# Block 1's projections from x times the norm's weight, with 1/std at the evictions, and the neighbourhood attention's values head by head in column halves

## What is computed

```
# block 1
h = x * rsqrt(mean(x*x, channels) + eps) * mix_norm_g
q, k, v, g, u, sv = split(h @ w_in)             # 4 heads of 128 and 4 groups of 128
q, k = rotary(q), rotary(k)
ret = silu(g) * rmsnorm(retention(q, k, v))     # chunks of 128 positions
sgu = gelu(u) * (w_s @ layernorm(gelu(sv)) + b_s)
x = x + concat(ret, sgu) @ w_out                # then a feed-forward part

# block 2, neighbourhood attention: 8 heads of 64, a grid of 16 rows and 64 columns
for each grid row r (64 queries):
    p = softmax(q_row @ k_window.T * scale + bias)   # 8 rows of 64 keys
    out[r] = p @ v_window
```

## Time and profile before

| | us |
|---|---|
| median of 3 runs (3180.71 to 3182.11) | 3181.14 |
| the profiled execution | 3180.48 |
| its span, first to last instruction | 3179.2 |
| TensorE busy | 3003.6 (94%) |
| VectorE busy | 1780.6 (56%) |
| ScalarE busy | 1150.5 (36%) |

### The profile page before, as it was taken

How to read it: one execution, slowest core, us unless ns; L and a number is a source line. 1 busy time by engine, 2 the same in 40 slices (tenths; PEclk the granted TensorE clock), 3 DMA queues, 4 the chain that set the end, 5 groups by cost and what they waited for, 6 DMA issues and landing times.

```text
span 3179.2 us, 34027 instructions
## 1 busy us (share of the span) xinstructions
PE 3003.6 (94%) x13986; PEld 2355.1 (74%) x13986; DVE 1780.6 (56%) x2535; ACT 1150.5 (36%) x1708; POOL 2.2 (0%) x6
## 2 busy tenths in 40 slices
PE   7999798999999997999998989999988899999997
PEld 5887687888888875877775757665556688888885
DVE  4442336444454447676774453667663866666666
ACT  3223413222222225344445434555642522222223
POOL 0000000000000000000000000000000000000000
PEclk9999999999999998999999999999989999999999
DMA  3211011111111111111110111000001111111111
GB/s 136 79 59 44 30 47 40 47 47 48 52 49 51 44 49 34 40 40 33 34 33 20 33 33 34 28 21 27 21 20 40 34 47 53 60 47 54 58 49 66
DMA packets 48823, 141.61 MB, mean 45 GB/s; under 512 B 12790, under 2 KB 16670, under 8 KB 48542
## 3 DMA queue, kind: packets, MB, share of 16 engines
q1 hardware_dynamic: 48670, 139.45, 14.0%
HBM read 135.16 MB, written 9.77 MB: 46 GB/s over the span
## 4 chain that ended last, share of the span: by engine, by line
PE 85%; ACT 6%; DVE 5%; issue 3%; DMA 0%; SPq 0%; ACTq 0%; DVEq 0%
PE psum L508 37%; PE psum L744 13%; PE psum L974 10%; PE psum L784 8%; PE psum L542 5%; PE psum L564 2%; PE psum L553 2%; PE psum L901 1%; PE psum L884 1%; PE psum L1056 1%; PE psum L1083 1%; PE psum L559 1%; DVE residual L1940 1%; ACT sb_left L1769 1%; DVE swa_p L2539 0%
## 5 line engine op out<-in xcount | busy, mean ns | idle before, releaser
L508 PE MATMUL psum<-h_hi,w_hi 128*128 128x512 f32 x1408 | 438.6, 393 | 6.6 <-ACT ret_q L1261 2.9
L508 PE MATMUL psum<-h_hi,w_lo 128*128 128x512 f32 x1408 | 434.0, 389 | 0.0
L508 PE MATMUL psum<-h_lo,w_hi 128*128 128x512 f32 x1408 | 434.0, 389 | 0.0
L1925 DVE TENSOR_TENSOR w_lo<-w_raw,w_hi 128x1024 fp32r<-128x1024 f32 x164 | 200.4, 1222 | 255.9 <-ACT w_hi L1168 255.5
L508 PEld LDWEIGHTS psum<-h_hi,w_hi 128*128 128x128 f32 x1408 | 262.8, 188 | 65.8 <-issue 13.0
L508 PEld LDWEIGHTS psum<-h_lo,w_hi 128*128 128x128 f32 x1408 | 264.3, 188 | 55.3
L508 PEld LDWEIGHTS psum<-h_hi,w_lo 128*128 128x128 f32 x1408 | 264.3, 188 | 55.2
L2166 DVE TENSOR_TENSOR residual<-residual,psum 128x1024 f32<-128x1024 f32 x176 | 214.5, 1219 | 141.6 <-PE psum L784 70.3
L1168 ACT ACTIVATE w_hi<-w_raw 128x1024 fp32r<-128x1024 f32 x164 | 172.5, 1052 | 227.3 <-PE psum L508 181.7
L974 PE MATMUL psum<-h_hi,w_hi 128*128 128x512 f32 x576 | 211.6, 447 | 5.2 <-ACT y L1180 2.3
L974 PE MATMUL psum<-h_hi,w_lo 128*128 128x512 f32 x576 | 204.1, 414 | 0.0
(11 more groups left out here) (332 smaller groups left out, 5256.4 us busy)
## 6 DMA issues: line engine op xcount, KB each, us to landing
w_raw<-in_weights SPq DMA_DIRECT2D x228, 512.0 KB, 3.5
residual<-in_x_t SPq DMA_DIRECT2D x8, 512.0 KB, 9.2
out_t<-residual SPq DMA_DIRECT2D x8, 512.0 KB, 3.0
rel_copies<-rel_rows SPq DMA_DIRECT2D x8, 480.0 KB, 6.2
na_bias<-rel_copies SPq DMA_DIRECT2D x8, 240.0 KB, 4.1
band_copies<-band_rows SPq DMA_DIRECT2D x8, 192.0 KB, 6.2
ret_rotary<-in_rotary SPq DMA_DIRECT2D x1, 1024.0 KB, 7.5
swa_bias<-band_copies SPq DMA_DIRECT2D x4, 256.0 KB, 2.8
```

The lines of the kernel that those rows point to most:

```text
L508: ins = self.pe.matmul(out[:, s], w[:, k, at:at + P], src(k, low)[:, s], start=(k == 0 and part == 0), stop=(k == n_k - 1 and part == 2))
L1925: self.dve.tensor_tensor(self.m.w_lo[:, n % 2, :], self.m.raw[:, n % 2, :], self.m.w_hi[:, n % 2, :].bitcast(F32), ALU.subtract).then_inc( ...
```

## The change

**First norm.** h_hi and h_lo are made from x * g, without 1/std, as x lands. The squares are summed over the eight tiles by VectorE; TensorE takes one mean of the sum (two matmuls, 4 passes) in the middle of tile 2. The loads start with the vectors and weight tiles 0 and 1; the constants come behind x. The rotary tables are multiplied by 1/std, and every other projection of block 1 is multiplied by 1/std by VectorE as it leaves PSUM; Silu and Gelu follow in place.

**Order.** Tiles 2 and 3 (v and gate of head 0) are projected straight behind the first pair, into banks 4 to 7. So head 0's three later projections are q, k and v of head 1, and head 1 has no value projection of its own at its start. VectorE multiplies the gate of heads 1 to 3 before it makes w_lo of the next tile.

**Values of the neighbourhood attention.** Each head is multiplied by itself, into its half of the partitions, and eight grid rows fill bank 7. ScalarE empties it with one operation.

```
 SyncE, program
+        sp.dma_start(m.vec[:], t["vectors"])
         for k in range(KD):
+            if k < 2: self.load_up_to(k)
             sp.dma_start(m.x[:, k, :], x[:, k, :])
+        sp.dma_start(m.common[:], t["common"])
         self.load_up_to(3); rotary; self.biases()
+        self.band()                      # was the end of biases()

 ScalarE, first_norm
+        self.split_up_to(0)
         for k in range(KD):
+            self.act.activation(m.h_hi[:, k, :], m.x[:, k, :], ACT.Copy, scale=m.v("mix_norm_g", k))
+            if k == 0: self.split_up_to(1)
+            if k > 2: q.wait_ge(*on("dve_n1_acc", k - 2))
             self.act.activation(dst[:], m.x[:, k, :], ACT.Square)
+        self.split_up_to(3)
         self.rsqrt(... m.n1_rstd, ("pe_n1_mean",), ("act_n1_rstd",))

 VectorE, first_norm
+        for k in range(KD):
+            self.dve.scalar_tensor_tensor(m.h_lo[:, k, :], m.x[:, k, :], m.v("mix_norm_g", k), m.h_hi[:, k, :], mult, subtract)
+            if k == 0: self.split_up_to(1)
+            if k > 1: self.add_first(k - 1)         # n_acc += squares
+        self.add_first(KD - 1)

 VectorE, retention
+        band add; self.split_up_to(3)
+        for n in range(2): m.rot[:, n, :] *= m.n1_rstd       # waits act_n1_rstd
         self.rotary(m.rq, 0, ...); self.rotary(m.rk, 1, ...)
+        self.values(0); self.times_rstd(m.rgate, 3, ("dve_rgate", 0))
         for h in range(RET_HEADS):
             t = 4 * h + 2
-            self.split_up_to(t + 1)
+            self.split_up_to(t + 1 if h else t + 2)
+            if h: self.values(h)                    # rt = proj t times 1/std
             rmask (waits pe_rscore); rqd
+            if h: self.times_rstd(m.rgate, t + 1, ("dve_rgate", h))
-            self.split_up_to(t + 2)
+            self.split_up_to(t + 2 if h else t + 3)
             state chain (waits pe_rkv) ...
             dve_rn (waits act_rrstd h); dve_ry

 TensorE, retention
         project_pair(...); band
+        for t, name in ((2, "dve_rv"), (3, "dve_rgate")):
+            out = self.take(("proj", t), 4 + 2 * (t - 2), 2, (name, 0))
+            for k in range(KD):
+                if t == 2 and k == 2: mean of m.n_acc into banks 6-7      # waits dve_n1_acc 7
+                ... six passes
         for h in range(RET_HEADS):
-            self.project(("act_rv", h))
+            if h > 1: self.project(("dve_rv", h))
             rkT, rscore, rvT (waits dve_rv h)
-            self.project(("act_rgate", h))
+            self.project(("dve_rgate", h) if h else ("dve_rq_cos", 1))
             rkv
+            self.project((q of h + 1) if h else ("dve_rk_cos", 1))
             ro
+            self.project((k of h + 1) if h else ("dve_rv", 1))
             rmean

 VectorE, gating
+                q.wait_ge(*on("pe_svT", g)); self.times_rstd(m.rk, t + 1, ("dve_sv", g + 1))
             smix; sy
+                self.after("dve_sy", g); self.times_rstd(m.rq, t, ("dve_u0", g + 1))

 TensorE, na_out
-        if r % 4 == 0: take bank 7
+        if r % 8 == 0: take bank 7
+        at = (r % 8) * GRID_W
         for b in range(4):
-            self.pe.matmul(self.n_out[:, (r % 4) * P:(r % 4 + 1) * P], m.nvtok[:, ks + 2 * b, :],
-                           m.npt[r % 2][:, b * P:(b + 1) * P], ...)
+            for a in range(2):
+                c = slice(64 * a, 64 * a + 64)
+                self.pe.matmul(self.n_out[c, at:at + GRID_W], m.nvtok[:, ks + 2 * b, c],
+                               m.npt[r % 2][:, b * P + 64 * a:b * P + 64 * a + 64], ...)

 ScalarE, na_out (every 8 rows, was every 4)
+        self.act.activation(m.y[:, p + 4, (r - 7) * GRID_W:(r + 1) * GRID_W], m.place["pe_nout", p, r // 8], ACT.Copy)
```

More of the change, by code:

```diff
@@ L603, in retention @@
         pe.matmul(out[0:SWA_HEADS, 0:REL_BAND], rel, onehot, start=True, stop=True).then_inc(*to("pe_band"))
+        for t, name in ((2, "dve_rv"), (3, "dve_rgate")):
+            q.wait_ge(*on("w_lo", t))
+            out = self.take(("proj", t), 4 + 2 * (t - 2), 2, (name, 0))
+            for k in range(KD):
+                if t == 2 and k == 2:
+                    q.wait_ge(*on("c_loaded"))
+                    q.wait_ge(*on("dve_n1_acc", KD - 1))
+                    mean = self.take(("pe_n1_mean",), 6, 2, ("act_n1_rstd", 1))
+                    for half, s in halves():
+                        pe.matmul(mean[:, s], m.c("mean1024"), m.n_acc[:, s], start=True, stop=True).then_inc(
+                            *to("pe_n1_mean", half))
+                w_hi, w_lo = self.weights(t)
+                for part, (w, low) in enumerate(((w_hi, 0), (w_lo, 0), (w_hi, 1))):
+                    for half, s in halves():
+                        ins = pe.matmul(out[:, s], w[:, k, :], self.h(k, low)[:, s], start=(k == 0 and part == 0),
+                                        stop=(k == KD - 1 and part == 2))
+            ins.then_inc(*to("proj", t))
+            self.tile += 1
         for h in range(RET_HEADS):
-            self.project(("act_rv", h))
+            if h > 1:
+                self.project(("dve_rv", h))
             q.wait_ge(*on("dve_rk", h))
@@ L1418, in neighbourhood @@
                 self.na_turn(step - 1)
-            if step >= 2 and (step - 2) % 4 == 3:
+            if step >= 2 and (step - 2) % 8 == 7:
                 self.na_out(step - 2)
@@ L2015, in retention @@
         dve.tensor_tensor(band, band, m.place[("pe_band",)][0:SWA_HEADS, 0:REL_BAND], ALU.add).then_inc(*to("dve_band"))
+        self.split_up_to(3)
+        q.wait_ge(*on("rotary_loaded"))
+        q.wait_ge(*on("act_n1_rstd", 1))
+        for n in range(2):
+            ins = dve.tensor_tensor(m.rot[:, n, :], m.rot[:, n, :], m.n1_rstd, ALU.mult)
+        ins.then_inc(*to("dve_rot"))
+        self.after("dve_rot")
+        self.rotary(m.rq, 0, "dve_rq", 0)
+        self.rotary(m.rk, 1, "dve_rk", 0)
+        self.values(0)
+        self.times_rstd(m.rgate, 3, ("dve_rgate", 0))
         for h in range(RET_HEADS):
             t = 4 * h + 2
-            self.split_up_to(t + 1)
+            self.split_up_to(t + 1 if h else t + 2)
+            if h:
+                self.values(h)
             q.wait_ge(*on("pe_rscore", h))
@@ L2028, in retention @@
             dve.tensor_tensor(chunks(m.rqd[:]), chunks(m.rq[:]), in_chunks(qdec), ALU.mult).then_inc(*to("dve_rqd", h))
-            self.split_up_to(t + 2)
+            if h:
+                self.after("dve_ry", h - 1)
+                self.times_rstd(m.rgate, t + 1, ("dve_rgate", h))
+            self.split_up_to(t + 2 if h else t + 3)
             q.wait_ge(*on("pe_rkv", h))
@@ L2053, in retention, with times_rstd, values @@
             dve.tensor_tensor(m.y[:, h, :], m.y[:, h, :], m.rgate[:], ALU.mult).then_inc(*to("dve_ry", h))
+    def times_rstd(self, dst, t, told):
+        self.q.wait_ge(*self.on("proj", t))
+        self.dve.tensor_tensor(dst[:], self.m.place["proj", t], self.m.n1_rstd, ALU.mult).then_inc(*self.to(*told))
+    def values(self, h):
+        self.after("dve_rk", h)
+        self.times_rstd(self.m.rt, 4 * h + 2, ("dve_rv", h))
     def gating(self):
@@ L2771, in program @@
         for k in range(KD):
+            if k < 2:
+                self.load_up_to(k)
             sp.dma_start(m.x[:, k, :], x[:, k, :]).then_inc(*landed(f"x{k}_loaded"))
+        sp.dma_start(m.common[:], t["common"]).then_inc(*landed("c_loaded"))
         self.load_up_to(3)
@@ L2817, in biases, with band @@
         sp.dma_start(t["rel_rows"], padded).then_inc(*landed("rel_rows_put"))
+    def band(self):
+        sp, q, t, on, landed = self.sp, self.q, self.t, self.on, self.landed
+        band = self.m.y[:, KD - 2, :][0:SWA_HEADS, REL_PAD + REL_BAND:REL_PAD + 2 * REL_BAND]
         q.wait_ge(*on("dve_band"))
```

146 lines of the change are left out of this document (75 added, 71 removed).

## The result

The changed kernel takes 3164.2 us (median of 5 runs, 3162.9 to 3165.2) against 3180.7 (3179.0 to 3182.1) of the kernel before, run beside it: a ratio of 0.9948, 95% interval 0.9935 to 0.9961, so 16.5 us faster.

A forecast was written before the change was run, and what follows sets the result against it. TensorE, with 85% of the chain that ended last, bounds the kernel. Gains of 9.4 (block 1), 5.8 (column halves) and 0.9 (last rows) sum to 16.1 us: 3180.5 becomes 3164.4, plus 0.7 for the median, 3165.1; range 3157 to 3176.

The forecast's parts named there:

- Start of the pair: Block 1's first pair of projections on TensorE would start at 13.1 us instead of 32.5: 19.4 us gained.
- Slow passes: At the start TensorE would stay at half clock somewhat longer than before: 0.4 us lost.
- Head 1: Waits before head 1's scores (1.1 us) and value transposes (1.85), uncovered behind head 0's mean: 3.0 us lost.
- w_lo: Heads 1 to 3: low weight part ready later behind the gate's product on VectorE, 1.2 us three times: 3.5 lost.
- Gating: Waits at group 0's first mean (0.9), for u's bank (0.1 three times) and in the last group (1.2): 2.4 us lost.
- given back: Rival, chance 0.14: block 1 loses half its 9.4 us to unfound VectorE queue waits or clock falls, giving 3170.
- Block 1 in all: Sum of the earlier start and all new waits in block 1: 9.4 us gained.
- Column halves: Neighbourhood attention values: 0.10 us saved a row after the way in and back, over 58 rows: 5.8 us gained.
- The last rows: Last attention rows: ScalarE's eviction leaves the chain of the convolution's squares that TensorE waits for: 0.9 us gained.
- the halves go by instructions: Rival, chance 0.11: in the 64 value groups a pair of halves takes 0.110 us, giving 3190.6, slower than before.
- The way back is cheap: Rival, chance 0.12: returning from halves to the full array costs 0.10, not 0.20 us, 5.8 more gained: 3159.
- The earlier start doesn't come: Rival, chance 0.03: x and weight loads share a queue, so the first pair starves: 3175.

The follow-up runs named there:

- the run with the mean inside the projection: Changed kernel with head 0's mean placed inside the projection of head 1's values, not behind it: 3160.9 us, 3.3 less.
- the halves alone: Kernel before with only the column halves of the neighbourhood attention's values: 3174.8 us, ratio to the kernel before 0.9983.
- the run with 128 columns: Changed kernel with each pass in column halves moving 128 columns, not 64, half the result unused, evictions as before: 3188.1 us, 23.9 more.
- block 1 alone: Changed kernel with the neighbourhood attention's values computed as before (full array, 128 columns): 3170.0 us, ratio to the kernel before 0.9968.
- two rows together: Changed kernel with the value passes of two grid rows together every second row, ahead of the transposes: 3156.5 us, 7.7 less.
- one more group: Changed kernel with each grid row's 16 value passes split into two groups of 8, one behind the next background passes: 3181.1 us, 16.9 more.

## Why the prediction was right

The time, 3165.1 against 3164.2, came in the main by the steps named. That it came so close is luck: the terms as they were measured come to less than was said, and 2.4 us behind the attention, which no term of the forecast had, made up for most of it.

- *Start of the pair: 19.4 said, 21.0 came.* Tile 0 had landed at 5.17, not at 7.0. The estimate took off the 449 KB of constants at 426 GB/s, 1.1 us, but it was 2.9. In the kernel before, the rate from 2 to 8 us is 329, 234 and 365 GB/s in stretches of 2 us; that explains some 1.5 us of the 2.9, and the rest is open. The chain behind it (table load, three operations on ScalarE, then h_lo and w_lo on VectorE) took 6.3 us, where 6.1 was said.
- *Slow passes: -0.4 said, -1.05 in this trace* (from the pair's start to the band's matmul 24.64 us, 23.59 before). Over the eight traces with that start the mean is 24.1, and the two with the old start have 23.6 and 23.8. So -0.4 to -0.5 was right for a run at large, and the rest is this execution's.
- *The mean inside tile 2 and the rotary's wait*, -1.7 and +1.5: both as said, and no wait before tile 2. *Head 0*: -0.6 for -0.5.
- *Head 1*: -3.0 said; 1.1 and 1.86 came, at the two places named, and the run with the mean inside the projection removed them. *w_lo*: -3.5 said, 3 x 1.2 came, and the order of two operations was shown as their cause.
- *Gating*: -2.4 said; -2.6 up to the last group's second mean (TensorE waits for u's bank twice, not three times, and 0.2 us longer each time), and 0.9 more by the granted clock, which falls at that mean. In the kernel before, and with the halves alone, the starts of its four passes lie within 1.4 us; in all eleven traces with the change of block 1, within 2.3 to 2.7. This was the rival "given back" in small. It falls whether the wait is 3.75 or 3.08 us; what would keep it up was not found.
- Block 1 in all: 9.4 said; in the trace 9.9 ahead of that mean's clock, 8.8 where block 2 begins and 8.5 at the first row; 10.6 timed alone. One trace can't tell this better: in the five traces whose code is the same up to that row the lead there is 7.9 to 10.8 (mean 9.4). They differ in the slow passes at the start, and in how long TensorE stays at the lower clock behind that mean (in the changed kernel 13.6 us there and 13.7 at the next norm, in the run with 128 columns 23.9 and 6.8).
- *Column halves: 0.10 a row said, 0.08 to 0.09 came.* A pair of halves takes 0.058 (0.055 said), the way in 0.15 (0.15), the way back 0.20 (0.20). The ways in and out came from the stick-breaking rows, at 128 columns and beside other work, and held here. Up to row 56, with 54 groups done, the lead grows by 4.8, where the forecast's price gives 5.4.
- *The last rows: +0.9 said, 0.5 at most came, and the clock took 0.9.* The evictions are gone from ScalarE, but TensorE's waits for the convolution and its squares and 1/std are 4.4, 3.8 and 2.0 us, 10.2 in all, against 9.9 before. The 1.94 of the earlier trace rows was one late wait of three; less in front of it was more elsewhere. From row 56 to the pointwise projections the lead grows by 0.5, four more groups of the attention included. Then their first 24 passes last 7.89 us against 7.03, at the lower clock for longer. So from row 62 to the pointwise layer's mean it is 47.4 us for 46.8. The table of windows over that work, of before and of after (the clock is the last number but two):

```profile
1724.00:1754.00 30.00, 25.61 (x104) 20.05 (x103) 11.45 (x10) 23.67 (x26) 0.00 (x0) 0.94 0.12 36
```

```profile
1711.00:1741.00 30.00, 25.61 (x100) 19.99 (x100) 10.68 (x9) 22.78 (x24) 0.00 (x0) 0.89 0.12 36
```

- *What was not foreseen: 2.9 us behind the attention*, where the code is the same. From the pointwise layer's mean to the next norm's projections the kernel before has 146.15 us and block 1 alone 146.25; the ten kernels with 64-column halves have 143.1 to 143.4 and that with 128-column halves 143.7. So it comes with the halves, wherever the rest stands in time. TensorE's waits in it are the same, the granted clock is not: at its lower level TensorE stands for 18.4 us of that stretch in the kernel before and for 11.1 in the changed kernel. The time is gained at three places behind a wait: 24 passes of the projections 8.53 us before and 7.41 after, the eight passes of a mean 5.40 and 5.17, the 32 of a norm's sum 15.53 and 13.97. From there to the end 0.5 is lost again. The table of windows of before (two lines), then of after, over the same work:

```profile
1754.00:1816.00 62.00, 54.55 (x214) 41.92 (x213) 30.84 (x27) 31.64 (x39) 0.00 (x0) 0.92 0.10 34
...
1867.00:1917.00 50.00, 37.67 (x103) 22.02 (x102) 36.93 (x35) 33.56 (x34) 0.00 (x0) 0.86 0.03 11
```

```profile
1741.00:1801.00 60.00, 52.55 (x210) 40.31 (x209) 30.67 (x26) 30.78 (x38) 0.00 (x0) 0.94 0.12 36
...
1851.00:1901.00 50.00, 37.66 (x110) 22.82 (x109) 36.83 (x35) 33.45 (x34) 0.00 (x0) 0.90 0.05 17
```

What in the attention moves the stretches at the lower clock is open. With the 0.9 lost just ahead and the 0.5 at the end, 1.5 us of the halves' gain is clock and not passes; it made up for the terms that came short.

Of the rivals, "the halves go by instructions" was the one to fear, and the run with 128 columns shows that it is false: the same instructions took 24 us more with twice the columns. (Its turning point, 0.088 us a pair, should be 0.090 by its own sum; nothing hangs on it.) "The way back is cheap" is false too: it is 0.20 into passes of 512 columns. Into the transposes it is 0.15 (0.259 from end to end against 0.109 behind a background pass), which is why two rows together gained about 0.4 and not 0.34. "The earlier start doesn't come" is false by the first pass at 11.51.

## What to carry to other kernels

Work in a part of the array costs a fixed way in and back, here 0.15 and 0.15 to 0.20 us, the same for groups of 4, 8 and 16 pairs. Count the groups first, and put groups together before making each shorter: here that alone was worth half as much as the whole change, and one way more in each row took all of it. When an engine takes over an eviction, write down what stands behind it in its queue: 3.6 us went to an order of two operations. A mean or another short step whose result is needed late belongs inside a projection, not between two: that gave 3.3 us here. And a forecast that comes out to the microsecond is to be checked place by place all the same: here 2.9 us came from a clock that the sum did not have in it.

## What the runs showed of the hardware

- The start: 6 to 13 passes took up to 0.43 us each, twice their 0.23, while the column of the granted clock read 1.00 (10.00:18.00 above). In the kernel before, from 32 to 36 us, passes of the same length go with a reading of 0.50. The reason lies in the trace: its first record of the clock stands at 17.2 us in the changed kernel and at 13.9 to 17.8 in the other twelve, within 0.2 us of the end of the slow passes, and the column shows 1.00 where there is no record. A kernel's first microseconds are to be read by the passes, not by that column.
- Their number differs by 7 passes, 1.4 us, between executions with nearly the same start: a term of that size at the start can't be read from one trace.
- The lower clock behind a wait can move with work that lies far ahead of it: 18.4 us of it against 11.1 in the same 143 to 146 us of code, by what the attention before it does. A difference of 1 to 3 us in unchanged code is to be looked for there first.
- Passes with 64 moving columns in two column halves keep 0.058 us a pair, with two weight loads and two matmul passes in it. The Trainium skill ("TensorEngine Tiling (Array Packing)", Key Properties) says that a change of tiling mode drains TensorE. The runs agree that the change has a price: with two rows together and with one more group they give it in this kernel from both sides, 0.29 us for one way in and back to the transposes, and with a way back to passes of 512 columns the rows give 0.34.
